# Attention step: mask and row extremum fused on VectorE, scores of the first four query blocks issued in pairs

## The chip, the cores and the metric

One core of a Trainium2 chip runs the whole layer. The metric is device time in microseconds, the median of the runs; the kernel before took 1771.34 us (three runs, 1770.96 to 1772.16).

## The reference

The reference computes one decoder layer in float32 for 1024 tokens and a model width of 1024. The part that matters here is differential causal attention with 8 heads. Each head has two maps (c = 0, 1) of 64 query and key channels and one value of 128 channels:

```python
sc = jnp.einsum('bhcqd,bhckd->bhcqk', q_blk, kt)       # q_blk: 128 queries, two maps
sc = jnp.where(k_pos[None, :] <= q_pos[:, None], sc, -jnp.inf)
p = jax.nn.softmax(sc, axis=-1)
p_diff = p[:, :, 0] - lam * p[:, :, 1]
o = jnp.einsum('bhqk,bhkv->bhqv', p_diff, vt)          # then RMSNorm per head
```

Before it come an RMSNorm and one wide projection, beside it a convolution, a pooling and three gates, and after it the output projection and a gated feed-forward block.

## The kernel before

Every float32 product is made of three fp32r products of high and low parts (the three PASSES: high by high, high by low, low by high). The program is written by hand for each engine: each engine has its own list of instructions in a fixed order, and semaphores tie the lists together. There is no planner; the order of the calls is the order on the engine.

Attention is a loop over heads, and within a head over eight steps, one for each query block i (a "row" of 128 queries that sees 128(i+1) keys). Head 0 and head 7 stand outside of the loop, heads 1 to 6 in it, two to a turn. Row i belongs to step i, but its stages are spread over several steps so that all engines work side by side.

- TensorE (`step_of`, and `scores` at L2440): the score products of row i; then the transposes of the difference of row i-1 (`diff_transposed`, L2348); then a quarter of a projection of the next head's keys or queries (`proj_part`, L2424, twelve products of 512 columns); then weights times values for row i-2 (L2462, L2464); then the transpose of the output y of row i-4 (L2348). A score product uses 64 rows of the array, rows 0 to 63 for map 0 and rows 64 to 127 for map 1; all the others use 128 rows.
- PSUM: map c has banks 2c and 2c+1. Rows 0 to 3 have at most 512 keys and use bank 2c alone; rows 4 to 7 use both, with three passes into the first and three into the second. `scores` waits for both exponentials of the row before (`exp_done`).
- VectorE (`step_of`): `masked` (L1669) waits for the scores and adds the triangular mask to the last 128 columns of both maps in one instruction, in place in PSUM, and waits for it; `maximum` (L1672) is called for each map and writes the negated row maximum over all 128(i+1) columns to `neg_max`. Then y of row i-3 (L1680), the low parts of the transposed row i-1 (L1559), and `difference` (L1657, L1658, L1662): reciprocals of the sums, a scale, and map 0 plus scale times map 1, into the tile `diff`. Splits of the next weights and low parts of projections (L1648) lie between the rows. The mask is a constant tile of 2 x 128 columns that GpSimd makes early in the kernel (L684, L685).
- ScalarE (`exps`, L1084): for each map the exponential of the scores plus `neg_max`, with the sum of the row from its accumulator, into `e_t`, which has two buffers (by i mod 2). Ahead of it in the same step ScalarE copies the high parts of the transposed row i-1.
- GpSimd computes the scale of the output norm from the sum of squares of u and moves values and outputs.

Of the kernel before, what the change touches and what calls it, by code (L numbers as in the profile page):

```python
# [12 lines left out]
P = 128  # L13
HALF = 512
EPS = 1e-6
MASKED = -1e30
WINDOWS = (2, 4, 8, 16)
# [55 lines left out]
def build(nc, x, g_pre_mix, w_in, b_gate, lambda_q1, lambda_k1, lambda_q2, lambda_k2, subln_g,  # L73
# [29 lines left out]
    with ctx:  # L103
# [72 lines left out]
        e_t = at("e_t", [P, 2, 2, S], F32, RF)  # L176
        diff = at("diff", [P, 2, S], F32, RF + 16384)
        gates_raw = at("gates_raw", [P, 2, S], F32, R2 + 16384)
# [35 lines left out]
        ident = const("ident", [P, P])  # L214
        mask = const("mask", [P, 2, P])
        bias_g = const("bias_g", [P, 3 * KT])
# [25 lines left out]
        def proj_weights(which, par, s):  # L242

            if which or not par:
                return ring[:, which, s, :]
            return k_other[s][:, :]

        def proj_bank(first, part):
# [33 lines left out]
        proj_done, proj_hi, proj_lo = sem("proj_done"), sem("proj_hi"), sem("proj_lo")  # L282
        scores_done, max_ready, exp_done = sem("scores_done"), sem("max_ready"), sem("exp_done")
        diff_ready = sem("diff_ready")
        u_lo_ready, u_ready = sem("u_lo_ready"), sem("u_ready")
# [344 lines left out]
        def _(pool):  # L630
# [16 lines left out]

            did(pool.memset(mask[0:1, 0, :], 1.0))
            did(pool.memset(ident[:, :], 0.0))
# [32 lines left out]

            for c in range(2):
                did(pool.memset(mask[:, c, :], 0.0))  # L684
                pool.affine_select(out=mask[:, c, :], in_=mask[:, c, :], compare_op=ALU.is_ge, fill=MASKED,  # L685
                                   base=0, pattern=[[-1, P]], channel_multiplier=1).then_inc(mask_ready, 1)
                pool.wait_ge(mask_ready, c + 1)
            store_v(TT - 2)
# [268 lines left out]
        def _(act):  # L957
# [120 lines left out]
            def exps(i, c):  # L1078

                w = P * (i + 1)  # L1080
                act.wait_ge(max_ready, t.at() * 2 + (c + 1))

                wait_for(act, diff_ready, t.at(-1))
                act.activation(e_t[:, i % 2, c, 0:w],  # L1084
                               ps[:, 2 * c:2 * c + 2, :].rearrange("p a b -> p (a b)")[:, 0:w], ACT.Exp,
                               bias=neg_max[:, i % 2, c:c + 1], accum_out=sums[:, i % 4, c:c + 1])\
                    .then_inc(exp_done, 1)
# [458 lines left out]
        def _(dve):  # L1546
# [106 lines left out]
            def difference(i, ahead=None):  # L1653
# [6 lines left out]
                if ahead:  # L1660
                    ahead()
                dve.scalar_tensor_tensor(diff[:, b, 0:w], e_t[:, b, 1, 0:w], d_scale[:, b:b + 1],  # L1662
                                         e_t[:, b, 0, 0:w], ALU.mult, ALU.add).then_inc(diff_ready, 1)

            def masked(i):

                dve.wait_ge(scores_done, t.at(1))
                block = ps[:, i // 4:i // 4 + 3:2, P * (i % 4):P * (i % 4 + 1)]
                did(dve.tensor_tensor(block, block, mask[:, :, :], ALU.add))  # L1669

            def maximum(i, c):
                dve.tensor_reduce(neg_max[:, i % 2, c:c + 1],  # L1672
                                  ps[:, 2 * c:2 * c + 2, :].rearrange("p a b -> p (a b)")[:, 0:P * (i + 1)],
                                  AX_X, ALU.max, negate=True).then_inc(max_ready, 1)

# [16 lines left out]
            def step_of(par, i, lag=0, first=False, last=False):  # L1692
                if not lag:
                    masked(i)
                    maximum(i, 0)
                    maximum(i, 1)
                if lag < 4 and not (first and i < 3):
# [36 lines left out]
            for half in range(2):  # L1734
                proj_lo_of(0, 1, half, first=True)
            dve.wait_ge(mask_ready, 2)
            for b in range(4):
                dve.wait_ge(v_stored[b], 16 * TT)
            for i in range(TT):
                step_of(0, i, first=True)  # L1740
            with turns(dve, (HEADS - 2) // 2, {n: 4, r: 4, p: 8, t: 16, trs: 40, step: 48}):
                for par in (1, 0):
                    for i in range(TT):
                        step_of(par, i)
# [574 lines left out]
        def _(pe):  # L2319
# [68 lines left out]
            for half in range(2):  # L2388
                pe.matmul(ps[:, 2 + half, :], mask[0:1, 0, :], g_pre_mix_b[0:1, HALF * half:HALF * (half + 1)],
                          start=True, stop=True).then_inc(g1_landed, 1)  # L2390
# [41 lines left out]
            def scores(par, i):  # L2432

                wait_for(pe, exp_done, t.at() * 2)
                for chunk in range(i // 4 + 1):
                    w = min(HALF, P * (i + 1) - HALF * chunk)
                    for n_pass, (a, b) in enumerate(PASSES):
                        for c in range(2):
                            rows = slice(HD * c, HD * (c + 1))
                            last = pe.matmul(ps[:, 2 * c + chunk, 0:w], qt[rows, par, a, P * i:P * (i + 1)],  # L2440
                                             kt[rows, par, b, HALF * chunk:HALF * chunk + w],
                                             start=n_pass == 0, stop=n_pass == 2)
                last.then_inc(scores_done, 1)

            def diff_transposed(i):
                pe.wait_ge(diff_ready, t.at())
                for b in range(i // 4 + 1):
                    blocks = min(4, i + 1 - 4 * b)
                    transpose_rows(b, diff[:, i % 2, HALF * b:HALF * b + P * blocks], blocks)

# [21 lines left out]
            def step_of(par, i, first=False):  # L2472
# [3 lines left out]
                if i == 4:  # L2476
                    pe.wait_ge(proj_lo, p.at(-2))
                scores(par, i)

# [305 lines left out]
```

## Time and profile before

| | |
|---|---|
| median of the runs | 1771.34 us |
| span of the profiled execution | 1769.8 us |
| TensorE busy | 1758.9 us (99%) |
| VectorE busy | 1151.7 us (65%) |
| ScalarE busy | 739.1 us (42%) |
| GpSimd busy | 250.7 us (14%) |

The page shows of the profiled execution its span, from the first to the last instruction; the runs are timed without a profile and from the outside, so that the two are not the same number. PE is TensorE, PEld its loading of weights, DVE is VectorE, ACT is ScalarE, POOL is GpSimd. L1672 is line 1672 of the kernel. A row of the timeline is a start in us from the beginning of the span, a duration, and what ran, where neighbours of one kind are put together (x6); a number in brackets is idle time before it and what ended it. A matmul's duration includes the way through the array, so that matmuls overlap and only the distance between starts tells how long a group takes.

### The profile page before, as it was taken

Reading aid. Unit: us, or ns where it says so; the run is one execution under the profiler, and the core shown is the slowest. Engines: PE = TensorE matmul, PEld = TensorE weight load, DVE = VectorE, ACT = ScalarE, POOL = GpSimd, SP = SyncE. Lnnn points to the kernel's source line nnn. Section 1 sums busy time; section 2 is a strip of 40 time slices with the busy share of each in tenths; the row PEclk is TensorE's granted clock in tenths of the full one; section 3 lists DMA queues with packets and bytes.
Section 4 is the critical chain, followed back from the end, with each engine's and each line's share of the span. In section 5 each row is a group of like instructions: output and inputs, shape, how many; then the busy total and the mean of one; then the engine's idle time right before and its main releaser. Section 6 shows DMA issues by size and latency. Waiting matters only on the chain.

```text
span 1769.8 us, 25045 instructions
## 1 busy us (share of the span) xinstructions
PE 1758.9 (99%) x8497; PEld 1455.0 (82%) x8497; DVE 1151.7 (65%) x1863; ACT 739.1 (42%) x1486; POOL 250.7 (14%) x557
## 2 busy tenths in 40 slices
PE   9999999999999999999999999999999999999998
PEld 7887888888888888888888888888888888888886
DVE  5328989999885774443465655776665655567676
ACT  5316666666743323443231123343333333344553
POOL 3221222222120001111100102101010000000011
PEclk9999999999999999999999999999999999999999
DMA  7421222222142222326735712223232322673443
GB/s 242 144 84 49 72 73 71 72 71 71 51 145 87 88 65 99 128 101 230 251 108 168 247 60 95 96 95 126 106 107 102 117 89 94 232 280 98 147 142 125
DMA packets 138041, 213.68 MB, mean 121 GB/s; under 512 B 7569, under 2 KB 94097, under 8 KB 136930
## 3 DMA queue, kind: packets, MB, share of 16 engines
q1 hardware_dynamic: 109200, 108.54, 19.4%
q0 software_dynamic: 28752, 104.04, 16.2%
q8 instruction: 46, 0.75, 0.2%
q14 instruction: 41, 0.34, 0.1%
q10 hardware_dynamic: 2, 0.00, 0.0%
HBM read 150.17 MB, written 62.39 MB: 120 GB/s over the span
## 4 chain that ended last, share of the span: by engine, by line
PE 98%; DVE 1%; issue 0%; ACT 0%; DMA 0%; POOL 0%; DVEq 0%; POOLq 0%; ACTq 0%
PE ps L2340 26%; PE ps L2672 22%; PE ps L2540 17%; PE ps L2728 12%; PE ps L2424 11%; PE ps L2440 4%; PE ps L2348 3%; PE ps L2462 2%; PE ps L2464 1%; DMA x_tile<-in_x_dram 0%; DVE pt L1559 0%; DVE ring L1559 0%; DVE neg_max L1672 0%; DVE ps L1669 0%; ACT e_t L1084 0%
## 5 line engine op out<-in xcount | busy, mean ns | idle before, releaser
L2728 PE MATMUL ps<-d_op 128*128 128x512 f32 x924 | 210.3, 389 | 0.1
L2728 PEld LDWEIGHTS ps<-d_op 128*128 128x128 f32 x924 | 173.3, 188 | 36.9 <-DVE d_op L1559 0.5
L2672 PE MATMUL ps<-s_op,t_op_T 128*128 128x512 f32 x720 | 169.9, 389 | 0.0
L2424 PE MATMUL ps<-xn,ring 128*128 128x512 f32 x672 | 167.1, 398 | 0.0
L2672 PEld LDWEIGHTS ps<-s_op,t_op_T 128*128 128x128 f32 x720 | 135.2, 188 | 28.0
L2424 PEld LDWEIGHTS ps<-xn,ring 128*128 128x128 f32 x672 | 122.5, 188 | 24.8 <-issue 0.2
L2540 PE MATMUL ps<-s_op,x_op_T 128*128 128x512 f32 x576 | 135.9, 389 | 0.0
L2540 PEld LDWEIGHTS ps<-s_op,x_op_T 128*128 128x128 f32 x576 | 108.1, 188 | 22.4
L2672 PE MATMUL ps<-hn,t_op_B 128*128 128x512 f32 x480 | 115.1, 389 | 0.0
L2672 PEld LDWEIGHTS ps<-hn,t_op_B 128*128 128x128 f32 x480 | 90.1, 188 | 18.7
L1084 ACT ACTIVATE e_t<-ps,neg_max 128x256 f32<-128x256 f32 (+7 forms) x128 | 94.1, 740 | 16.5 <-DVE neg_max L1672 15.1
L1559 DVE TENSOR_TENSOR t_op_B<-pair,t_op_B 128x512 fp32r<-128x512 f32 x60 | 41.4, 689 | 90.8 <-ACT t_op_B L963 90.8
L963 ACT ACTIVATE d_op<-rf_pieces 128x512 fp32r<-128x512 f32 x87 | 53.8, 629 | 106.6 <-PE ps L2728 101.1
L1559 DVE TENSOR_TENSOR d_op<-rf_pieces,d_op 128x512 fp32r<-128x512 f32 x87 | 59.3, 691 | 59.9 <-ACT d_op L963 59.9
L1672 DVE TENSOR_REDUCE neg_max<-ps 128x1 f32<-128x256 f32 (+7 forms) x128 | 91.0, 752 | 2.2
L2540 PE MATMUL ps<-xn,x_op_B 128*128 128x512 f32 x384 | 92.1, 389 | 0.0
L2340 PE MATMUL ps<-w_v,xn 128*128 128x512 f32 x384 | 90.5, 395 | 0.0
L2340 PE MATMUL ps<-w_o,ring 128*128 128x512 f32 x384 | 89.0, 391 | 0.0
L2340 PE MATMUL ps<-ya,ring 128*128 128x512 f32 x384 | 87.8, 389 | 0.0
L2340 PEld LDWEIGHTS ps<-w_v,xn 128*128 128x128 f32 x384 | 72.4, 190 | 15.1 <-DVE xn L1559 0.3
L2540 PEld LDWEIGHTS ps<-xn,x_op_B 128*128 128x128 f32 x384 | 72.1, 188 | 14.9
L2340 PEld LDWEIGHTS ps<-ya,ring 128*128 128x128 f32 x384 | 72.1, 188 | 14.9
(270 smaller groups left out, 3374.7 us busy)
## 6 DMA issues: line engine op xcount, KB each, us to landing
pair<-in_w_gate_up_dram SPq DMA_DIRECT2D x20, 1024.0 KB, 5.2
rf_pieces<-s_scratch SPq DMA_DIRECT2D x74, 256.0 KB, 2.7
x_pair<-in_w_in_dram SPq DMA_DIRECT2D x16, 1024.0 KB, 6.2
raw<-in_w_in_dram SPq DMA_DIRECT2D x26, 512.0 KB, 4.0
s_scratch<-gated_ff POOLq DMA_DIRECT2D x40, 256.0 KB, 2.5
gate_in<-gate_scratch POOLq DMA_DIRECT2D x18, 512.0 KB, 3.8
v_scratch<-v_out POOLq DMA_DIRECT2D x32, 256.0 KB, 2.6
vh<-v_scratch POOLq DMA_DIRECT2D x16, 512.0 KB, 5.3
```

The source lines that it names most:

```text
L963: return act.activation(dst, src, ACT.Copy, **kw)
L1084: act.activation(e_t[:, i % 2, c, 0:w], ps[:, 2 * c:2 * c + 2, :].rearrange("p a b -> p (a b)")[:, 0:w], ACT.Exp, bias=neg_max[:, i % 2, c ...
L1559: return dve.tensor_tensor(dst, src, hi.bitcast(F32), ALU.subtract)
L1672: dve.tensor_reduce(neg_max[:, i % 2, c:c + 1], ps[:, 2 * c:2 * c + 2, :].rearrange("p a b -> p (a b)")[:, 0:P * (i + 1)], AX_X, ALU.max, ...
L2340: last = pe.matmul(ps[:, bank, :], lhs, rhs, start=i == 0, stop=i == len(pairs) - 1)
L2348: last = pe.transpose(ps[:, TB[b], P * k:P * (k + 1)], src[:, P * k:P * (k + 1)], ident[:, :])
L2424: last = pe.matmul(ps[:, proj_bank(first, half), :], proj_weights(which, par, a)[:, P * k:P * (k + 1)], xn[:, b, k, HALF * half:HALF * (ha ...
L2440: last = pe.matmul(ps[:, 2 * c + chunk, 0:w], qt[rows, par, a, P * i:P * (i + 1)], kt[rows, par, b, HALF * chunk:HALF * chunk + w], start= ...
L2462: pe.matmul(ps[:, U_BANK, 0:2 * HV], pt[:, i % 2, HH, k, :], vh[:, par, :, k, :], start=k == 0, stop=k == i, skip_group_check=True)
L2540: last = pe.matmul(ps[:, bank, :], x_op[name][:, a, k, :], block(b, k), start=opens and (k, a, b) == (0, HH, HH), stop=(k, a, b) == (3, LL ...
L2672: last = pe.matmul(ps[:, bank, :], t_op[name][:, a, k, :], block(b, k), start=opens and (k, a, b) == (0, HH, HH), stop=(k, a, b) == (3, LL ...
L2728: last = pe.matmul(ps[:, DOWN_BANKS[product][i], :], d_op[:, g % 4, a, P * i:P * (i + 1)], d_op[:, g % 4, 2 + b, :], start=opens and (a, b ...
```

## The change

- Scores of rows 0 and 1 are issued at step 0, one behind the other, and those of rows 2 and 3 at step 2; steps 1 and 3 issue none. Rows 0 and 2 keep bank 2c, rows 1 and 3 now use bank 2c+1 (`score_row`). The wait for the exponentials of the row before stands ahead of each of the two, with the same value. `scores_done` is counted up after each row.
- `masked` and `maximum` become `minimum`, one VectorE instruction for each map: the scores plus a mask over the full width of the row, times -1, written back in place, and the minimum of the result as the negated maximum. ScalarE's exponential takes the negated scores with a scale of -1.
- The mask becomes one row of 1024 columns, zero but for the last 128; it takes the place in memory of the tile `diff`, and GpSimd makes it once the last normalised input rows have been read out of that place. The difference is written over the first map in `e_t`.
- A row of ones that TensorE reads in the first microseconds gets a tile of its own.

```diff
-        diff = at("diff", [P, 2, S], F32, RF + 16384)
+        mask = at("mask", [P, S], F32, RF + 16384)
...
+        def score_row(i, c):
+            first = 2 * c + (i % 2 if i < 4 else 0)
+            return ps[:, first:2 * c + 2, :].rearrange("p a b -> p (a b)")[:, 0:P * (i + 1)]
...
-            for c in range(2):
-                did(pool.memset(mask[:, c, :], 0.0))
-                pool.affine_select(out=mask[:, c, :], in_=mask[:, c, :], compare_op=ALU.is_ge, fill=MASKED,
-                                   base=0, pattern=[[-1, P]], channel_multiplier=1).then_inc(mask_ready, 1)
-                pool.wait_ge(mask_ready, c + 1)
+            pool.wait_ge(rows_ready, TT + 1)
+            did(pool.memset(mask[:, :], 0.0))
+            pool.affine_select(out=mask[:, S - P:S], in_=mask[:, S - P:S], compare_op=ALU.is_ge, fill=MASKED,
+                               base=0, pattern=[[-1, P]], channel_multiplier=1).then_inc(mask_ready, 1)
...
                 act.activation(e_t[:, i % 2, c, 0:w],
-                               ps[:, 2 * c:2 * c + 2, :].rearrange("p a b -> p (a b)")[:, 0:w], ACT.Exp,
-                               bias=neg_max[:, i % 2, c:c + 1], accum_out=sums[:, i % 4, c:c + 1])\
+                               score_row(i, c), ACT.Exp,
+                               bias=neg_max[:, i % 2, c:c + 1], scale=-1.0, accum_out=sums[:, i % 4, c:c + 1])\
...
-                dve.scalar_tensor_tensor(diff[:, b, 0:w], e_t[:, b, 1, 0:w], d_scale[:, b:b + 1],
+                dve.scalar_tensor_tensor(e_t[:, b, 0, 0:w], e_t[:, b, 1, 0:w], d_scale[:, b:b + 1],
                                          e_t[:, b, 0, 0:w], ALU.mult, ALU.add).then_inc(diff_ready, 1)
 
-            def masked(i):
-                dve.wait_ge(scores_done, t.at(1))
-                block = ps[:, i // 4:i // 4 + 3:2, P * (i % 4):P * (i % 4 + 1)]
-                did(dve.tensor_tensor(block, block, mask[:, :, :], ALU.add))
-
-            def maximum(i, c):
-                dve.tensor_reduce(neg_max[:, i % 2, c:c + 1],
-                                  ps[:, 2 * c:2 * c + 2, :].rearrange("p a b -> p (a b)")[:, 0:P * (i + 1)],
-                                  AX_X, ALU.max, negate=True).then_inc(max_ready, 1)
+            def minimum(i, c):
+                if c == 0:
+                    dve.wait_ge(scores_done, t.at(1))
+                    dve.sem_inc(scores_seen, 1)
+                w = P * (i + 1)
+                scores = score_row(i, c)
+                dve.tensor_tensor_reduce(out=scores, in0=scores, in1=mask[:, S - w:S], scale=-1.0, scalar=HIGHEST,
+                                         op0=ALU.add, op1=ALU.min, accum_out=neg_max[:, i % 2, c:c + 1])\
+                    .then_inc(max_ready, 1)
...
-                            last = pe.matmul(ps[:, 2 * c + chunk, 0:w], qt[rows, par, a, P * i:P * (i + 1)],
+                            last = pe.matmul(score_row(i, c)[:, HALF * chunk:HALF * chunk + w], qt[rows, par, a, P * i:P * (i + 1)],
...
-                scores(par, i)
+                if i >= 4 or i % 2 == 0:
+                    scores(par, i)
+                if i < 4 and i % 2 == 0:
+                    scores(par, i + 1)
```

## Rows read from the trace of the kernel before

**Rows 1.** The page: busy time of each engine; shares of the chain by engine.
```profile
PE 1758.9 (99%) x8497; PEld 1455.0 (82%) x8497; DVE 1151.7 (65%) x1863; ACT 739.1 (42%) x1486; POOL 250.7 (14%) x557
...
PE 98%; DVE 1%; issue 0%; ACT 0%; DMA 0%; POOL 0%; DVEq 0%; POOLq 0%; ACTq 0%
```

**Rows 2.** Busy time by stretch: head 0, and one head of the loop.
```profile
core 0: us, PE busy (x) PEld busy (x) DVE busy (x) ACT busy (x) POOL busy (x), PEclk, DMA share, GB/s
132.00:174.00 42.00, 41.04 (x257) 33.45 (x255) 37.30 (x80) 26.36 (x72) 7.40 (x20) 1.00 0.18 51
...
352.00:396.50 44.50, 44.39 (x286) 36.93 (x288) 40.36 (x91) 29.12 (x82) 9.96 (x27) 1.00 0.22 71
```

**Rows 3.** Waits of PE: us in total, times, longest.
```profile
PE ps L2440 <- ACT e_t L1084: 0.2, 1, 0.2
PE ps L2348 <- DVE diff L1662: 0.2, 1, 0.2
```

**Rows 4.** Timeline of PE, head 5 and start of 6: start us, duration us, what.
```profile
361.46 0.30 PE L2348 MATMUL ps<-ident,y_row 128*128 128x128 f32 x1
...
362.58 0.55 PE L2348 MATMUL ps<-ident,diff 128*128 128x128 f32 x3
...
367.52 0.66 PE L2348 MATMUL ps<-ident,diff 128*128 128x128 f32 x4
...
371.55 0.29 PE L2348 MATMUL ps<-ident,y_row 128*128 128x128 f32 x1
...
373.00 0.77 PE L2348 MATMUL ps<-ident,diff 128*128 128x128 f32 x5
...
383.44 0.29 PE L2348 MATMUL ps<-ident,y_row 128*128 128x128 f32 x1
...
385.25 0.98 PE L2348 MATMUL ps<-ident,diff 128*128 128x128 f32 x7
...
392.35 1.03 PE L2348 MATMUL ps<-ident,diff 128*128 128x128 f32 x8
393.13 0.71 PE L2424 MATMUL ps<-xn,k_other_hi 128*128 128x512 f32 x2
...
396.16 0.28 PE L2348 MATMUL ps<-ident,y_row 128*128 128x128 f32 x1
396.37 0.62 PE L2440 MATMUL ps<-kt,qt 64*128 64x256 f32 x6
396.93 0.33 PE L2348 MATMUL ps<-ident,diff 128*128 128x128 f32 x1
```

**Rows 5.** Timeline of DVE: row 3 of head 5, row 0 of head 6.
```profile
363.46 0.42 DVE L1669 TENSOR_TENSOR ps<-ps,mask 128x256 f32<-128x256 f32 x1
363.91 1.29 DVE L1672 TENSOR_REDUCE neg_max<-ps 128x1 f32<-128x512 f32 x2
...
366.63 0.75 DVE L1662 SCALAR_TENSOR_TENSOR diff<-e_t,d_scale 128x512 f32<-128x512 f32 x1
...
395.99 0.35 DVE L1662 SCALAR_TENSOR_TENSOR diff<-e_t,d_scale 128x128 f32<-128x128 f32 x1
```

**Rows 6.** Groups of instructions of DVE by line and shape: busy us, mean ns.
```profile
L1559 DVE TENSOR_TENSOR pt<-ps,pt 128x512 fp32r<-128x512 f32 x48 | 32.1, 683 | 0.0
L1669 DVE TENSOR_TENSOR ps<-ps,mask 128x256 f32<-128x256 f32 x64 | 27.3, 427 | 9.8 <-PE ps L2440 6.5 <-issue 3.1
...
L1672 DVE TENSOR_REDUCE neg_max<-ps 128x1 f32<-128x512 f32 x16 | 10.3, 685 | 0.3
...
L1662 DVE SCALAR_TENSOR_TENSOR diff<-e_t,d_scale 128x1024 f32<-128x1024 f32 x8 | 10.2, 1276 | 0.0
```

**Rows 7.** Groups of ACT by line and shape, attention alone.
```profile
L1084 ACT ACTIVATION_READ_ACCUMULATOR e_t<-ps,neg_max 128x1 f32 x126 | 24.7, 196 | 0.0
```

**Rows 8.** Timeline of POOL where the mask is made.
```profile
85.75 0.20 POOL L684 MEMSET mask<- 128x128 f32 x1
...
90.70 0.57 POOL L659 DMA_DIRECT2D v_scratch<-v_out  x1 [3.59 <-DVE v_out L1559]
```

More of the change, by code:

```diff
@@ L15 @@
 EPS = 1e-6
+HIGHEST = 3.0e38
 MASKED = -1e30
@@ L214, in build @@
         ident = const("ident", [P, P])
-        mask = const("mask", [P, 2, P])
+        ones = const("ones", [P, P])
         bias_g = const("bias_g", [P, 3 * KT])
@@ L283, in build @@
         scores_done, max_ready, exp_done = sem("scores_done"), sem("max_ready"), sem("exp_done")
+        scores_seen = sem("scores_seen")
         diff_ready = sem("diff_ready")
@@ L646, in rstd_of @@
                                    ALU.pow).then_inc(rstd_ready, 1)
-            did(pool.memset(mask[0:1, 0, :], 1.0))
+            did(pool.memset(ones[0:1, :], 1.0))
             did(pool.memset(ident[:, :], 0.0))
@@ L1693, in step_of @@
                 if not lag:
-                    masked(i)
-                    maximum(i, 0)
-                    maximum(i, 1)
+                    minimum(i, 0)
+                    minimum(i, 1)
                 if lag < 4 and not (first and i < 3):
@@ L1735, in _ @@
                 proj_lo_of(0, 1, half, first=True)
-            dve.wait_ge(mask_ready, 2)
+            dve.wait_ge(mask_ready, 1)
             for b in range(4):
@@ L1740, in _ @@
                 step_of(0, i, first=True)
-            with turns(dve, (HEADS - 2) // 2, {n: 4, r: 4, p: 8, t: 16, trs: 40, step: 48}):
+            with turns(dve, (HEADS - 2) // 2, {n: 4, r: 4, p: 8, t: 16, trs: 40, step: 32}):
                 for par in (1, 0):
@@ L2388, in _ @@
             for half in range(2):
-                pe.matmul(ps[:, 2 + half, :], mask[0:1, 0, :], g_pre_mix_b[0:1, HALF * half:HALF * (half + 1)],
+                pe.matmul(ps[:, 2 + half, :], ones[0:1, :], g_pre_mix_b[0:1, HALF * half:HALF * (half + 1)],
                           start=True, stop=True).then_inc(g1_landed, 1)
@@ L2448, in diff_transposed @@
                     blocks = min(4, i + 1 - 4 * b)
-                    transpose_rows(b, diff[:, i % 2, HALF * b:HALF * b + P * blocks], blocks)
+                    transpose_rows(b, e_t[:, i % 2, 0, HALF * b:HALF * b + P * blocks], blocks)
             def weighted_values(par, i, newer):
```

## The prediction

> **What bounds the kernel now.** I read the page first. TensorE is busy 99% of the span and is 98% of the chain that ended last [rows 1]; every other engine is covered, so a change pays only if it takes time out of TensorE's own stream or out of one of its few waits. Then the busy times by stretch: in one head of the attention loop (44.5 us) TensorE is busy 44.39, VectorE 40.36, and the granted clock is 1.00 throughout [rows 2]. VectorE is therefore second by only four microseconds and lies in a loop with TensorE: scores, mask, maximum, exponential, difference, transposes. The table of waits shows that TensorE waits for this loop almost nowhere; two waits of 0.2 us, for the exponentials and for the difference, are all that is booked on it [rows 3]. They belong to head 0: the first 42 us of attention hold 0.96 us of idle TensorE [rows 2].
>
> "Busy" hides something, which the timeline of TensorE shows. Score products use 64 rows of the array, everything around them 128. In step 1 the transpose of y starts at 396.16, the six products of 256 columns at 396.37, the next transpose at 396.93 [rows 4]: 0.77 us, though one transpose is 0.10 (eight of them fill 392.35 to 393.13) and three passes of 256 columns are 0.36 (below). So some 0.31 us is entering and leaving. Steps 5 and 7 show that this is paid once per group and not per bank: there twelve products in two banks follow each other, 371.55 to 373.00 = 1.45 us with a second half of 256 columns and 383.44 to 385.25 = 1.81 us with one of 512, against 1.12 us for the first half alone (361.46 to 362.58) [rows 4]. A second group thus costs 0.33 us at 256 columns and 0.69 us at 512, so 0.36 us for three passes of 256 columns.
>
> **The change, part by part.**
> *Scores in pairs.* Step 1 loses 0.77 - 0.10 = 0.67 us and step 0 gains 0.33: net 0.34. Step 3 loses 1.12 - 0.10 = 1.02 and step 2 gains 0.69: net 0.33. Per head 0.67 us, over eight heads 5.4 us, all on the path. The wait ahead of the pair is the old one of its first row (exponentials of the row before), so nothing is queued behind a new wait; the odd row has its own banks, so the products of row 1 don't touch what VectorE is reducing.
>
> *One VectorE instruction per row and map.* Before, a row costs the mask addition, 0.45 us from its start to the start of the first reduction (363.46 to 363.91), and two reductions [rows 5]. After, it is two fused instructions, each reading scores from PSUM and the mask from SBUF and writing back. An addition of that kind is in the trace: 427 ns for 256 columns in place, 683 ns for 512, a plain reduction 685 ns for 512 [rows 6]. So I price the pass itself as the reduction. Bringing the minimum out is not shown on VectorE. Bounds: from below nothing beyond the pass; from above 0.20 us each, the mean of ScalarE's accumulator read [rows 7]; far above, a second cycle per column (the second rival). I take 0.09 us, nearer to the lower end, as a read can overlap the next instruction's start. A row then saves 0.45 - 0.18 = 0.27 us, a head 2.2 us of 40.4. This is not on the path by itself; it pays for what follows.
>
> The Trainium skill ("VectorE: DVE Perf Modes", section on two Vector instructions with no wait between them) says that an operation with an accumulator output is two instructions, the main one and a read. No VectorE row here shows one; by it a row would hold four instructions in place of three, and at ScalarE's 0.20 us the saving would be 0.05 us a row, in place of 0.27.
>
> *What is late next.* Without the scores of row 1 ahead of them, the transposes of row 0 are wanted 0.67 us sooner: 4.58 - 0.67 = 3.91 us behind those of row 7 (392.35 to 396.93 before), while the difference of row 0 ended 395.99 + 0.35 = 396.34, 3.99 behind [rows 4, 5]. With some 0.1 us for the semaphore it is 0.2 late, unless the 0.27 us of row 0 and row 7 reach it. The second place is row 3: its difference ended 366.63 + 0.75 = 367.38, its transposes began at 367.52, 0.14 us spare [rows 4, 5]. TensorE comes there 0.67 us sooner; rows 0 to 3 give 4 x 0.27 = 1.1 us, but part of their chain is ScalarE and GpSimd, which don't get faster. I book 0.1 us of new waiting per head, from 0 to 0.35.
>
> *Head 0* is bound by VectorE's chain in its first steps, so there 0.27 us a row for four rows counts, 1.1 us; bounds 0.5 (mask saving of two rows) and 1.7 (0.96 us of idle time gone and 0.67 of TensorE's own).
>
> *At nothing:* the wide zero mask on GpSimd. A memset of 128 columns took 0.20 us; eight times that is 1.6 us at most, and GpSimd then idled 3.59 us before its next store [rows 8]; without that cover up to 1.6 us of a store would slip, still long before head 0. The difference in place writes as many columns as before; its buffer is overwritten by exponentials that ScalarE issues behind the copies of a later transpose, so no wait is added. The sign in the exponential is a constant of the instruction.
>
> **Sum.** 7 x (0.67 - 0.10) + 1.1 = 5.1 us. The profiled execution shows a span of 1769.8 us; it becomes 1764.7. The median of the runs, 1771.34, lies 1.5 us above that span, and I keep this: 1766.2 us.
>
> **Rivals.**
> 1. *TensorE's saving turns into waits.* If reading the minimum costs 0.2 us or more, VectorE gains nothing, and the two late places eat 0.2 to 0.5 of the 0.67 us per head; the same result would come if the second row of a pair paid the entry again. For: 0.14 us spare at row 3. Against: 0.45 us is surely gone from each row, and the two-bank groups of steps 5 and 7. Time: 8 x 0.17 to 8 x 0.4 saved at the far end, 1768.1 to 1771; around 1770.
> 2. *The fused instruction is slow, and VectorE becomes the bound.* An addition, a scaling and a running minimum per column could take two cycles. Additions cost (683 - 427)/256 = 1.0 ns a column [rows 6]; a head has 2 x 4608 columns, 9.2 us more, less the 2.2 us of above: VectorE at 47.4 us a head, with one to four microseconds of its present idle time left 48.4 to 51, against 44.4 now. Over eight heads 32 to 53 us: about 1805. It decides from the price at which VectorE's head passes TensorE's: 40.4 - 3.6 (the masks) + 16x = 43.7, x = 0.43 us above a reduction. The Trainium skill ("Vector Engine (DVE) Microarchitecture Reference", points that are easy to get wrong) says that the scalar-tensor-tensor shape with two non-bf16 SBUF sources runs at half throughput, with no port left for the accumulator. The difference is of this shape with two such sources, without an accumulator, and took 1276 ns for 1024 columns [rows 6]: not halved; and the scores are in PSUM.
> 3. *More than I book:* no waits at all and head 0 freed wholly: 7 x 0.67 + 1.7 = 6.4, with 0.3 for the roughness of the readings 6.7: 1764.6. This is the end of the gain, since TensorE can't give more than its entries.
>
> **Numbers.** Forecast, with rival 3: 0.66. Rival 1: 0.21. Rival 2, in all sizes: 0.13. A measurement here can tell 0.2% (3.5 us) from no change: faster beyond 1767.8, slower beyond 1774.9. Faster 0.67 (all but a little of the first case and some of rival 1), same 0.21, slower 0.12. The range goes from 1764.0, just below the end of the gain, to 1772.5, which takes in rival 1 and the start of rival 2.
>
> **What would show it.** Six score products followed by six more without a gap at steps 0 and 2, and the transposes of rows 0 and 2 directly behind that of y. Head period 43.8 us in place of 44.4. The fused instruction about 0.7 us at 512 columns and VectorE near 38 us a head. Wrong if: TensorE shows waits on the difference above 0.2 us a head (rival 1), or the fused instruction takes about 2 ns a column (rival 2), or the time outside attention moves by more than 0.5 us.

## The result and the profile after

The changed kernel is slower. Its median is 1775.76 us (10 runs, 1774.82 to 1776.78) against 1771.52 for the kernel before on the same chip: ratio 1.0023, 95% interval 1.0015 to 1.0031. The forecast was 1766.2 and the range 1764.0 to 1772.5: the measured time lies above its upper end. The profiled execution has a span of 1774.8 us, 5.0 more than before.

The page's busy row and the shares of the chain come first; they answer to [rows 1].

```profile
PE 1758.3 (99%) x8497; PEld 1456.9 (82%) x8497; DVE 1131.0 (64%) x1927; ACT 735.0 (41%) x1486; POOL 250.2 (14%) x555
...
PE 93%; DVE 3%; issue 2%; POOL 1%; ACT 1%; DMA 0%; POOLq 0%; DVEq 0%; ACTq 0%
```

VectorE is 20.7 us less busy, as wanted. But TensorE's share of the chain fell from 98% to 93%, and "issue", time in which an engine waited for nothing that the profile shows, rose from 0 to 2%. Where that lies is seen from the time between the starts of the transposes of row 7 of one head and the next (timeline of TensorE; heads 1 to 6 are in the loop, two to a turn, and heads 3 and 5 begin a new turn):

| head | 1 | 2 | 3 | 4 | 5 | 6 | 7 |
|---|---|---|---|---|---|---|---|
| before, us | 44.35 | 44.26 | 44.81 | 44.26 | 44.74 | 44.27 | 43.81 |
| after, us | 44.33 | 44.11 | 48.37 | 44.06 | 48.39 | 44.09 | 42.57 |

Heads 3 and 5 lose 3.56 and 3.65 us; head 7 gains 1.24, the rest of the loop 0.55 together, head 0 0.43 (to its row 7). The sum is 5.0 lost, the whole difference of the spans. From row 7 of head 7 to the end it is 1289.4 us in both kernels, so nothing moved outside of attention.

Busy times by stretch (columns as in [rows 2]), for head 4 and head 5:

```profile
306.30:350.40 44.10, 43.88 (x286) 36.96 (x285) 37.01 (x94) 28.70 (x82) 10.02 (x28) 1.00 0.23 72
350.40:398.80 48.40, 45.89 (x286) 38.15 (x285) 37.97 (x102) 28.81 (x82) 10.00 (x28) 0.96 0.21 66
```

VectorE needs 37 to 38 us a head, not 40.4. In head 5 TensorE has 2.5 us of idle time and the granted clock falls to 0.96. Waits of TensorE in heads 1 to 7, where the kernel before shows none:

```profile
PE ps L2353 <- DVE pt L1565: 3.6, 2, 1.8
PE ps L2353 <- DVE e_t L1668: 2.3, 8, 0.5
```

Timeline of VectorE where head 5 begins, and the chain of waits of the same stretch (start, duration, what):

```profile
349.48 0.28 DVE L1565 TENSOR_TENSOR y_out<-ps,y_out 128x128 fp32r<-128x128 f32 x1
354.11 0.30 DVE L1678 CUSTOM_DVE_ANT_0 ps<-ps,mask 128x128 f32<-128x128 f32 x1 [4.34 <-issue]
354.32 0.14 DVE L1678 DVE_READ_ACCUMULATOR2_ANT neg_max<- 128x1 f32 x1
354.32 0.33 DVE L1678 CUSTOM_DVE_ANT_0 ps<-ps,mask 128x128 f32<-128x128 f32 x1
```

```profile
349.76 1.84 issue
351.60 0.06 DVEq L51
351.66 2.29 issue
353.95 0.02 DVEq L1675
353.97 0.14 issue
354.11 0.25 DVE ps L1678
```

VectorE stands for 4.34 us at the loop's turn: 1.84 us to the loop's first instruction (L51), 2.29 more to its second (L1675). The kernel before stands 1.59 and 1.53 us there. The transfers in 256 to 264 us, around the other turn, are nothing but code:

```profile
q14 instruction: 3, 0.02, 1.1%
```

TensorE behind the turn of head 5:

```profile
354.13 0.23 PE L2469 MATMUL ps<-vh,pt 128*128 128x128 f32 x1
356.17 0.33 PE L2353 MATMUL ps<-ident,y_row 128*128 128x128 f32 x1 [1.81 <-DVE pt L1565]
357.01 0.32 PE L2353 MATMUL ps<-ident,e_t 128*128 128x128 f32 x1 [0.51 <-DVE e_t L1668]
357.09 4.58 PE L2429 MATMUL ps<-xn,ring 128*128 128x512 f32 x12
```

It idles 1.81 and 0.51 us, and then twelve products take 4.58 us that take 3.00 at a granted clock of 1.00 (experiment 1). Busy times by stretch for these products (the granted clock is the third number from the end):

```profile
357.09:361.50 4.41, 4.41 (x13) 3.47 (x14) 2.36 (x10) 2.51 (x8) 0.93 (x3) 0.61 0.00 0
```

A mean of 0.61 says that for most of this stretch TensorE had the lower of its two clocks (1.2 GHz, 0.50); ahead of it (from 353.90) and from 361.50 on it is 1.00. Waits and slower products are 2.32 + 1.58 = 3.90 us of the 4.12 that head 5 is longer than in the same kernel without the gap.

The fused instruction itself, by shape (busy us, mean ns), answers to [rows 6]:

```profile
L1678 DVE CUSTOM_DVE_ANT_0 ps<-ps,mask 128x1024 f32<-128x1024 f32 x16 | 19.3, 1248 | 6.5 <-PE ps L2445 6.5
L1678 DVE DVE_READ_ACCUMULATOR2_ANT neg_max<- 128x1 f32 x128 | 18.2, 142 | 0.0
...
L1678 DVE CUSTOM_DVE_ANT_0 ps<-ps,mask 128x512 f32<-128x512 f32 x16 | 10.7, 711 | 0.0
```

(1248 - 711)/512 = 1.05 ns a column, and the read of the accumulator is an instruction of its own, but the next operation starts with it (354.32 twice above).

### The profile page after: what moved, and what is told of

Read it like the earlier page. It is cut to its first block, busy times and chain, and to the rows that moved or that the text cites. A ratio compares the mean times of both kernels' runs of the same rounds, so it can differ in the third digit from the quotient of the medians.

```text
span 1774.8 us, 25115 instructions
## 1 busy us (share of the span) xinstructions
PE 1758.3 (99%) x8497; PEld 1456.9 (82%) x8497; DVE 1131.0 (64%) x1927; ACT 735.0 (41%) x1486; POOL 250.2 (14%) x555
## 4 chain that ended last, share of the span: by engine, by line
PE 93%; DVE 3%; issue 2%; POOL 1%; ACT 1%; DMA 0%; POOLq 0%; DVEq 0%; ACTq 0%
PE ps L2345 26%; PE ps L2680 21%; PE ps L2548 17%; PE ps L2736 11%; PE ps L2429 8%; PE ps L2353 3%; PE ps L2445 3%; PE ps L2467 2%; PE ps L2469 1%; DVE pt L1565 1%; POOL o_scale L727 0%; DVE e_t L1668 0%; DVE d_scale L1664 0%; DVE ring L1565 0%; DVE u_row L1693 0%
## 5 line engine op out<-in xcount | busy, mean ns | idle before, releaser
L1678 DVE CUSTOM_DVE_ANT_0 ps<-ps,mask 128x256 f32<-128x256 f32 (+7 forms) x128 | 94.5, 780 | 22.5 <-PE ps L2445 13.8
```

What stands on the lines that cost most here:

```text
L1678: dve.tensor_tensor_reduce(out=scores, in0=scores, in1=mask[:, S - w:S], scale=-1.0, scalar=HIGHEST, op0=ALU.add, op1=ALU.min, accum_out=n ...
```

## The experiments

The theory that the traces gave: the turn of VectorE's loop waits for code. In the compiled programs an instruction has 64 bytes, and the instruction queue moves 8 KB at a time, 128 instructions. The loop's body has 318 instructions before and 334 after, and the change puts 15 more ahead of it. A place is an instruction's number within its 8 KB, from 0 to 127. Where the 8 KB boundaries lie isn't in the profile; I assumed that the changed loop's first instruction is the last of its 8 KB (place 127), since its second came 2.29 us after it. The kernel before then starts at place 112, and all other places follow by counting. Experiments 1 to 4 bear the assumption out: with the two kernels they leave only 126 and 127 for it, if a loop is fetched anew where it touches four pieces and stays where it touches three. The rival: the fused instruction or the pairs make the gap themselves.

### 1. The changed kernel, loop shifted by two instructions

```diff
             dve.wait_ge(mask_ready, 1)
+            for _ in range(4):
+                dve.wait_ge(mask_ready, 1)
```

> The changed kernel with four more waits on VectorE ahead of the first head, on a semaphore value that is long there; they put two more instructions ahead of the loop over the heads and change nothing in it. Theory (placement of the code): in the changed kernel VectorE stands 4.33 and 4.34 us at the two loop turns (the kernel before: 1.59 and 1.53), because the loop body's first instruction is the last of one 8192-byte fetch and its second stands in the next. With the body moved to the head of a fetch, the gaps fall to 1.0 to 1.7 us, the transposes of row 7 of heads 3 and 5 come about 44.1 to 44.9 us after those of the head before (48.37 and 48.39 in the changed kernel), TensorE's granted clock is 0.99 or more in these heads, and the time is 1766.5 to 1769. Rival (the fused instruction or the pairs make these gaps, whatever the placement): gaps above 4 us and 1775 to 1776.5.

In the compiled program four such waits make two instructions. Measured: 1768.18 us (ratio to before 0.9980, 0.9971 to 0.9989). Heads 3 and 5 took 44.29 and 44.27 us. Timeline of VectorE at both turns, and the twelve products of TensorE behind the second:

```profile
257.25 0.28 DVE L1565 TENSOR_TENSOR y_out<-ps,y_out 128x128 fp32r<-128x128 f32 x1
257.45 0.29 DVE L1678 CUSTOM_DVE_ANT_0 ps<-ps,mask 128x128 f32<-128x128 f32 x1
...
345.60 0.28 DVE L1565 TENSOR_TENSOR y_out<-ps,y_out 128x128 fp32r<-128x128 f32 x1
345.79 0.29 DVE L1678 CUSTOM_DVE_ANT_0 ps<-ps,mask 128x128 f32<-128x128 f32 x1
```

```profile
356.95 3.00 PE L2431 MATMUL ps<-xn,ring 128*128 128x512 f32 x12
```

No gap is left, not even the 1.5 us of before: the theory was right on the time and too careful on the gap. Two instructions that do nothing are worth 7.6 us.

### 2. The kernel before, loop shifted to place 127

```diff
             dve.wait_ge(mask_ready, 2)
+            for _ in range(31):
+                dve.wait_ge(mask_ready, 2)
```

> The kernel before with 31 more waits on VectorE ahead of the first head, on a semaphore value that is long there: 15 more instructions in the queue, so that the loop's body begins at the place in VectorE's code that it has in the changed kernel. Theory (placement of the code): the two gaps at the loop turns go from 1.59 and 1.53 us to above 4, the two heads to about 48.5 us, and the time is 1777 to 1780. Rival (the changed instructions make the gaps): 1771 to 1772, as the kernel before.

Measured: 1779.78 us (ratio 1.0044, 1.0031 to 1.0057); heads 3 and 5 48.39 and 49.71. The added waits also delay head 0 by 1.6 us (its first transpose starts at 132.34 in place of 130.77), since VectorE is not idle there. First turn on VectorE:

```profile
259.78 0.28 DVE L1559 TENSOR_TENSOR y_out<-ps,y_out 128x128 fp32r<-128x128 f32 x1
263.99 0.43 DVE L1669 TENSOR_TENSOR ps<-ps,mask 128x256 f32<-128x256 f32 x1 [3.93 <-issue]
```

The old instructions make the long gap as well once their loop begins there, so the rival is ruled out. (The profiled execution was the longest of the five, 1782.19 us. Its second turn costs more than its first because TensorE had the lower clock for longer behind it: the granted clock is 0.66 in 356.5 to 366.5 us and 0.83 in 264 to 274 us.)

### 3. The kernel before, loop shifted to lie in three fetches

```diff
+            for _ in range(34):
+                dve.wait_ge(lam_landed, 16 * 5)
             for half in range(2):
                 proj_lo_of(0, 0, half, first=True)
```

> The kernel before with 17 more instructions on VectorE where it stands idle (ahead of the first projection), so that its loop begins one instruction behind the start of an 8192-byte fetch and lies in three of them instead of four. Nothing else is changed. Theory (the loop's code is fetched again at every turn only where it does not lie in three fetches): no fetch on the instruction queue between about 240 and 440 us, the gaps of 1.59 and 1.53 us at the two turns go, heads 3 and 5 take 44.3 us (44.81 and 44.74 before), and the time is 1770.3 to 1771. Rival (a turn costs 1.5 us in this kernel wherever its code lies): 1771.3 to 1772.

Measured: 1770.31 us; heads 3 and 5 44.32 and 44.33. The ratio, 0.9994 (0.9985 to 1.0003), does not tell the two kernels apart, but the heads do. VectorE at the second turn:

```profile
346.36 0.28 DVE L1559 TENSOR_TENSOR y_out<-ps,y_out 128x128 fp32r<-128x128 f32 x1
346.56 0.42 DVE L1669 TENSOR_TENSOR ps<-ps,mask 128x256 f32<-128x256 f32 x1
```

Between 256 and 440 us the instruction queue moved nothing, whereas in the kernel before, in the same stretch, it moved

```profile
q14 instruction: 10, 0.08, 0.1%
```

which is also where the 8 KB come from (0.08 MB in 10 packets).

### 4. The changed kernel, loop at place 53

Edit as in 3, with 108 waits (54 instructions) on the changed kernel.

> The changed kernel with 54 more instructions on VectorE ahead of the first projection (most of them where VectorE stands idle): the loop begins at place 53 of an 8192-byte fetch and reaches into a fourth. Theory: the code is fetched again at each turn, but the first fetch holds 75 instructions of the loop, so that only the first fetch is waited for and not two: gaps of 1.3 to 2.0 us as in the kernel before, heads 3 and 5 at 44.4 to 45.0 us, and 1768.5 to 1770 (up to 1 us more if the waits themselves delay the first head). Rival A (every fetch anew costs over 4 us in the changed kernel): 1775. Rival B (no fetch anew, gaps of 0.9): 1768.2 as the shifted changed kernel.

Measured: 1770.53 us; heads 3 and 5 45.29 and 45.21. VectorE at the first turn (from 256 to 440 us the instruction queue moved 11 packets):

```profile
260.01 0.30 DVE L1678 CUSTOM_DVE_ANT_0 ps<-ps,mask 128x128 f32<-128x128 f32 x1 [2.82 <-issue]
```

The code was fetched anew, as expected of a loop in four fetches, and VectorE waited for code once and not twice: the chain of waits has 2.56 us to the first instruction and 0.05 to the second. But the gap is 2.82 us where I expected 1.3 to 2.0, and the time is 0.5 us above my upper end. The chains of waits show most of the reason; here the kernel before and then this run (the first line is the branch back, the last the loop's first instruction):

```profile
257.16 0.06 DVEq L50
...
258.54 1.48 issue
260.02 0.06 DVEq L50
```

```profile
256.27 0.07 DVEq L51
...
257.19 2.56 issue
259.75 0.06 DVEq L51
```

From branch to first instruction it is 2.86 us before and 3.48 here, and in between one packet of code starts before and two here. Also VectorE, which still works off what it was given ahead of the branch, covers 1.38 us of it before (until 258.54) and only 0.92 here (until 257.19). Why two packets go out at this place is not shown. TensorE idled 0.29 and 0.51 us behind the turn, and its granted clock stayed at 1.00.

Places and gaps together:

| | place | 8 KB pieces touched | q14 packets, 256 to 440 us | gaps at the turns, us |
|---|---|---|---|---|
| before | 112 | 4 | 10 | 1.59, 1.53 |
| after | 127 | 4 | 10 | 4.33, 4.34 |
| 2, before | 127 | 4 | 10 | 3.93, 3.86 |
| 4, after | 53 | 4 | 11 | 2.82, 2.78 |
| 1, after | 1 | 3 | 0 | none |
| 3, before | 1 | 3 | 0 | none |

### 5. The pairs alone, and the fused instruction alone

The pairs on the kernel before; the odd row has banks of its own, chosen so that the mask's two blocks lie side by side:

```diff
-                scores(par, i)
+                if i >= 4 or i % 2 == 0:
+                    scores(par, i)
+                if i < 4 and i % 2 == 0:
+                    scores(par, i + 1)
...
+        def score_row(i, c):
+            if i < 4:
+                return ps[:, 2 * (i % 2) + c, 0:P * (i + 1)]
+            return ps[:, 2 * c:2 * c + 2, :].rearrange("p a b -> p (a b)")[:, 0:P * (i + 1)]
```

> The kernel before with the paired score products alone (the two products of a row pair lie in banks of their own as in the change; the mask addition and the two row maxima are as before). VectorE's code has the length of the kernel before, so its loop is placed as there. As the prediction booked the pairs: 0.67 us a head less on TensorE, 1771.5 less 5, 1766 to 1767. Theory now (the pairs shorten TensorE's steps 1 to 3, but these steps end on the VectorE chain that runs over the scaled row, the difference and the sum of the row): most of it comes back as waiting at the transposes, 1769.5 to 1771.5. Rival (pairs make the loop turns long): above 1775.

The kernel of experiment 1 with `scores(par, i)` at every step again:

> The changed kernel with the score products in the order of before (each row's pair of products at its own step), so the fused mask and minimum alone, with the four added waits, so that VectorE's loop is placed as in the shifted changed kernel. As the prediction booked it: VectorE is 0.27 us a row shorter, which lies beside TensorE's work except in the first head and the head outside the loop: 1769.5 to 1771.5. Rival (the fused instruction holds the rows up): slower than the kernel before, above 1772. Second rival (the shorter VectorE row alone carries the gain of the heads): 1767 to 1769.

Measured: the pairs alone 1772.07 us (ratio 1.0003, 0.9994 to 1.0011), no gain, 0.6 us above what I expected; the fused instruction alone 1768.76 (0.9984, 0.9975 to 0.9993), the second rival's range. With the pairs on top it is 1768.18 (experiment 1). So at equal placement the fused instruction gives 1.6 us (from the 1770.31 of experiment 3; the kernel before stood at 1771.66 and 1771.52 beside the two; by the spans of the profiled executions it is 1.2) and the pairs 0.6. Differences of this size lie within the intervals of the ratios; the heads carry the argument. Heads, in us:

| head | 1 | 2 | 3 | 4 | 5 | 6 | 7 |
|---|---|---|---|---|---|---|---|
| before, three fetches | 44.33 | 44.25 | 44.32 | 44.27 | 44.33 | 44.29 | 43.81 |
| pairs alone | 44.56 | 44.53 | 45.03 | 44.56 | 45.05 | 44.53 | 42.75 |
| fused alone | 44.19 | 44.19 | 44.19 | 44.19 | 44.19 | 44.19 | 43.60 |
| both (1) | 44.29 | 44.07 | 44.29 | 44.06 | 44.27 | 44.09 | 42.55 |

The pairs take 1.05 us out of head 7 and nothing worth naming out of a head in the loop. (Some 0.4 of the 1.05 is a shift: row 7 of a head now waits for one more row of the next head's scores, 7.51 us behind row 6 in place of 7.10, and behind head 7 there is no next head. The rest, 0.65, is the booked saving.) TensorE's waits in the pairs alone, heads 1 to 7:

```profile
PE ps L2354 <- DVE diff L1668: 1.6, 5, 0.6
PE ps L2446 <- ACT e_t L1090: 1.2, 6, 0.2
```

### 6. What eats the pairs in the loop

Steps 2 and 3 of head 4 on VectorE in experiment 1:

```profile
312.04 0.28 DVE L1693 TENSOR_TENSOR u_row<-ps,u_lo 128x128 f32<-128x128 f32 x1
...
314.20 0.35 DVE L1686 SCALAR_TENSOR_TENSOR y_row<-u_row,o_scale,g_sub 128x128 f32<-128x128 f32 x1 [0.63 <-POOL o_scale L728]
...
315.31 0.62 DVE L1668 SCALAR_TENSOR_TENSOR e_t<-e_t,d_scale 128x384 f32<-128x384 f32 x1
315.84 1.22 DVE L1565 TENSOR_TENSOR ring<-raw,ring 128x1024 fp32r<-128x1024 f32 x1
316.98 0.28 DVE L1693 TENSOR_TENSOR u_row<-ps,u_lo 128x128 f32<-128x128 f32 x1
...
319.14 0.35 DVE L1686 SCALAR_TENSOR_TENSOR y_row<-u_row,o_scale,g_sub 128x128 f32<-128x128 f32 x1 [0.36 <-POOL o_scale L728]
...
320.37 0.75 DVE L1668 SCALAR_TENSOR_TENSOR e_t<-e_t,d_scale 128x512 f32<-128x512 f32 x1
```

and the transposes that follow on TensorE:

```profile
321.26 0.65 PE L2355 MATMUL ps<-ident,e_t 128*128 128x128 f32 x4 [0.23 <-DVE e_t L1668]
```

From one u_row to the next it is 4.94 us: a square on ScalarE and three operations on GpSimd (o_scale) to y_row, then the difference, then the weight split `ring` of 1.22 us. The difference ends 0.13 to 0.14 us ahead of its transposes in rows 2 and 3, that is, they wait for it. Row 3's transposes come 5.20 us behind row 2's; in the kernel before and in the fused instruction alone it is 4.93. Two edits try the two suspects: y_row's wait, and the split.

```diff
-                if lag < 4 and not (first and i < 3):
-                    y_of((i - 3) % TT)
...
+                if lag < 4 and not (first and i < 3):
+                    y_of((i - 3) % TT)
                 if lag < 3 and not (first and i < 2):
                     sum_u((i - 2) % TT)
```

> The shifted changed kernel (the same two instructions more ahead of VectorE's loop, put where VectorE stands idle anyway) with one more edit: in every step the scaling that makes y_row stands behind the difference and the weight splits, just ahead of the sum for u_row, and no longer ahead of the difference. Theory (the pairs' saving turned into waiting at the transposes of rows 2 and 3, because y_row's wait on GpSimd's o_scale, 0.63 and 0.36 us there, stands ahead of the difference): the slack of 0.13 us at rows 2 and 3 grows, the transposes of rows 1 to 2 and 2 to 3 are 0.23 us (odd heads) and 0.2 to 0.3 us closer, a head takes 43.6 to 43.9 us instead of 44.06 and 44.29, and the time is 1765.5 to 1767. Rival (the exponentials, not y_row, end last at these rows): heads at 44.0 to 44.3 and 1768 to 1768.5. Other rival (y_row itself comes late for its transposes): above 1768.5.

> The paired score products alone on the kernel before, with the scaling that makes y_row moved behind the difference and the splits as in the run above; VectorE's code is placed as in the kernel before. Theory: the old mask addition and maximum leave VectorE 40 us busy of 44.5 in a head, so rows 2 and 3 still wait, but less: heads at 44.1 to 44.4 us instead of 44.53 and 44.56, 1769.5 to 1771. Rival (without the fused instruction the pairs cannot gain at all): 1771.8 to 1772.3, as the pairs alone.

Measured: 1767.60 us for the changed kernel with y_row moved (0.9977, 0.9968 to 0.9986), 1777.76 for the pairs alone with y_row moved (1.0035, 1.0021 to 1.0049). The first misses its range by 0.6, with heads at 44.09 to 44.15: the odd ones gained 0.15 to 0.2, the even ones nothing, and head 7 lost 0.3. Heads 1 to 7 together take 307.57 us, against 307.62 in experiment 1, so a gain from this edit is not shown. The second is wrong in sign: 5.7 us slower than without the edit, heads at 45.44 to 45.61. The reason stands in VectorE's row 3, here in the first of them,

```profile
318.29 0.55 DVE L1565 TENSOR_TENSOR pt<-ps,pt 128x384 fp32r<-128x384 f32 x1
319.29 0.17 DVE L1663 RECIPROCAL rsums<-sums 128x2 f32<-128x2 f32 x1 [0.46 <-ACT e_t L1090]
```

and here in the second:

```profile
321.44 0.35 DVE L1686 SCALAR_TENSOR_TENSOR y_row<-u_row,o_scale,g_sub 128x128 f32<-128x128 f32 x1
...
324.77 0.17 DVE L1663 RECIPROCAL rsums<-sums 128x2 f32<-128x2 f32 x1 [0.45 <-ACT e_t L1090]
```

y_row used to stand in time that VectorE had to wait anyway, for the exponentials. Moved out of it, its 0.27 us come on top (in the second kernel rows 2 and 3 come 0.22 and 0.26 us later behind the row before, rows 4 to 6 some 0.1 to 0.2), and the wait only changes its name from GpSimd to ScalarE. My single limit was two chains of nearly equal length, 4.94 us through o_scale, 5.11 through the exponentials (difference 314.70 to 319.81 in the first of the two). Both hold the split.

```diff
-                    if i == 2 and not last:
+                    if i == 6 and not last:
                         split_weights(0, par)
```

on ScalarE and VectorE alike.

> The shifted changed kernel with one more edit: the weight split that stands in step 2 behind the difference (1.22 us on VectorE, 1.06 on ScalarE) stands in step 6 instead, on both engines; y_row stands where the change has it. Theory (two chains end nearly together at row 3, one through GpSimd's o_scale and y_row, 4.93 us a row, and one through minimum, exponentials, difference, split and the next minimum, 5.11 us when y_row is moved; both hold the split of step 2): without the split in it the transposes of rows 2 to 3 are 4.9 us apart (5.20 in the shifted changed kernel, 4.88 in head 7, which has no split), the slack of row 3 grows from 0.13 to 0.4 or more, a head takes 43.5 to 43.9 us, and the time is 1765.3 to 1766.8. In step 6 the split falls into gaps of 0.93 us on VectorE and 1.11 on ScalarE. Rival (TensorE itself cannot run the paired order faster): tr rows 2 to 3 stays at 5.2 us and 1768. Other rival (the split in step 6 delays row 7): above 1768.5.

> The run above with y_row moved behind the difference too. Theory: row 2 of the odd heads gains the 0.23 us that it gained in the kernel with y_row alone moved, three heads; row 3 has its slack already: 0.3 to 0.8 us below the run above, 1764.8 to 1766.2. Rival (y_row in its new place adds 0.27 us to the rows that the exponentials end): as the run above or up to 0.5 us slower.

> The paired score products alone on the kernel before (old mask addition and maximum, VectorE's code placed as there), with the split of step 2 moved to step 6 on both engines. Theory: the pairs did nothing alone (1772.07) because rows 2 and 3 wait for VectorE; with 1.1 us less there they gain: heads at 43.9 to 44.3 us instead of 44.53 and 44.56, 1768.5 to 1770.5. Rival (the pairs need the fused instruction: VectorE's rows 4 to 7, now with the split among them, end last): 1771.5 or more.

> The fused mask and minimum alone (score products in the order of before, VectorE's loop placed to lie in three fetches), with the split of step 2 moved to step 6 on both engines. It is the control of the run with the pairs and the moved split. Theory (the moved split gives back the pairs' saving and has none of its own: without the pairs TensorE is busy 44.19 of 44.19 us in a head): heads stay at 44.1 to 44.3 us and the time is 1768.2 to 1769.3, as the fused instruction alone (1768.76). Rival (the moved split shortens the heads by itself): 1766 to 1767.5.

Measured: the changed kernel with the split in step 6: 1765.71 us (0.9966, 0.9954 to 0.9979), the fastest here and ahead of both kernels. With y_row moved as well 1767.15 (0.9977, 0.9967 to 0.9987), against my expectation: rows 6 and 7 of a head are 7.8 to 7.9 us apart in place of 7.6 (the rival's mechanism, at three times its price). The pairs alone with the split in step 6: 1769.68 (0.9990, 0.9981 to 0.9999). The control, without the pairs: 1769.43 (0.9986, 0.9977 to 0.9995), 0.7 above the fused instruction alone and 0.1 above my range: with the split in step 6 row 7 comes 0.1 us later in each head. The fastest kernel shows row 3 freed on VectorE (u_row now waits for ScalarE's copy of TensorE's product) and on TensorE (the difference ends 0.42 us ahead of its transposes), and a head filled by TensorE:

```profile
314.64 0.29 DVE L1693 TENSOR_TENSOR u_row<-ps,u_lo 128x128 f32<-128x128 f32 x1 [0.47 <-ACT u_lo L969]
...
318.05 0.75 DVE L1668 SCALAR_TENSOR_TENSOR e_t<-e_t,d_scale 128x512 f32<-128x512 f32 x1
```

```profile
319.22 0.65 PE L2355 MATMUL ps<-ident,e_t 128*128 128x128 f32 x4
```

```profile
304.60:348.30 43.70, 43.70 (x286) 36.84 (x285) 37.47 (x98) 28.90 (x82) 9.99 (x27) 1.00 0.22 72
```

Rows 2 to 3 are 4.92 us apart (314.30 to 319.22; 5.20 in experiment 1), and heads take 43.71 (even) and 43.95 to 44.00 (odd). The difference to the control, 3.7 us, is what the pairs give where VectorE lets them; against the fused instruction alone, which doesn't pay for the moved split, it is 3.1.

## Why the prediction was wrong

*The step that failed is the list of what the change costs.* "The change part by part" counts the instructions that VectorE executes and prices "at nothing" a memset, a buffer and a sign. It does not count the code: 15 instructions more ahead of the loop, 16 more in it. They moved the loop's first instruction from place 112 to 127, and at each of the two turns the time until VectorE goes on grew by 2.8 us; TensorE lost 8.2 us by it in heads 3 and 5 (48.37 and 48.39 against 44.29 and 44.27), 1.6 us of each head by the lower clock behind its idle time. Experiments 1 to 3 show it with the instructions changed and unchanged. The sign was in the rows: 3.1 us of "issue" ahead of the mask addition [rows 6], in two waits at the turns, were idle time of VectorE that no work explained, and I passed over them.

The Trainium skill ("Runtime: NRT & Kernel Launch", section "Instruction fetch mechanics") says that a taken branch to code outside the present window of two blocks waits for a fetch. The runs agree on the mechanism: 3 packets of code at a turn, and none where there is no gap. The Trainium skill gives a block 16 KiB, 256 instructions. The runs don't agree with that size: no alignment of blocks of 256 instructions puts the loops that were fetched anew (before, after, 2 and 4) into three blocks and the others (1 and 3) into two. Here the packets have 8 KB, and a loop in three of them stayed.

*The pairs: right in size, wrong in "what is late next".* The entries saved are there: the even heads of the fastest kernel take 43.71 us against 44.29 and 44.30 in its control, 0.6 where 0.67 was forecast, and head 7 shows 0.65. But "I book 0.1 us of new waiting per head" should have been about 0.6: at equal placement heads 1 to 6 take 44.18 us on average with the pairs and 44.19 without, and the pairs gave 0.6 us in all and not 4. Of the two late places named, row 0 cost nothing (3.95 us behind row 7, where 3.91 was reckoned), and row 3 (0.14 us spare) cost 0.3 in every head of the loop; row 4 cost 0.1 and row 2 of the odd heads 0.25. The price was wrong because I took VectorE's saving of 0.27 us a row to shorten the chain there in full. It does so in part: row 3 comes 5.20 us behind row 2 with the fused instruction and 5.38 without it, but from one u_row to the next it is 4.94 in both. One chain goes through GpSimd and the other through the exponentials, and the difference comes when the later of the two allows. This is rival 1's outcome by another mechanism; its condition, a read that costs 0.2 us, is not met.

*The fused row: right.* VectorE needs 37.5 us a head where "near 38" was forecast; the read of the accumulator is 142 ns long and lies beside the next operation. Rival 2 is out: 1.05 ns a column. The fused instruction gave 1.6 us, 0.5 in head 0 (38.64 us from its first transposes to those of row 7, 39.12 in experiment 3), where 1.1 was booked together with the pairs, and some 0.1 in each head of the loop, where nothing was.

*Of the signs named:* waits on the difference are 2.3 us in seven heads, above 0.2 a head, but two of 0.5 us stand behind the turns; at equal placement it is 1.3, just under 0.2. The head period is 44.1 (even) and 44.3 (odd), not 43.8. The time outside attention did not move. Without the placement the change would have stood at 1768.18, inside the range and 2 us above the forecast, but that would have been partly luck: 1.2 us of it are the turns of the kernel before (1771.52 to 1770.31), which the forecast did not count. At equal placement the change gives 2.1 us (1770.31 to 1768.18) where 5.1 were booked.

*What stays open:* why a turn at place 53 sends for two packets of code ahead of the loop's first instruction and one at place 112 for a single one; and why the odd heads of the fastest kernel take 0.25 us more than the even ones; it lies in row 2, and is gone where y_row is moved.

## What to carry to other kernels

A loop on an engine's queue has a place in its code, and any edit ahead of it or in it moves that place: look for idle time marked "issue" at the loop's turns and for packets on the instruction queue before comparing two versions, and place the loop alike in both. A saving on the engine that bounds the kernel counts only up to the next chain that ends at the same wait, and two chains of nearly equal length have to be shortened in what they share (here the split, 2.5 us) and not in the one that the profile happens to name (y_row: no gain that is shown, and 5.7 us lost on the pairs alone). An operation that stands in a wait that is there anyway costs nothing; moved out of it, it does.

## What the runs showed of the hardware beyond that

- Two instructions without effect made 7.6 us (1775.76 to 1768.18), because the loop of 334 instructions then touches three 8 KB pieces of code and not four, by the places counted above.
- Idle time of TensorE was paid twice: behind waits of 1.81 and 0.51 us the granted clock was 0.61 over twelve products, which took 4.58 us in place of 3.00. Behind waits of 0.29 and 0.51 us (experiment 4) it stayed at 1.00.
- A fused addition, scaling and running minimum over scores in PSUM took 1.05 ns a column, as an addition alone does [rows 6].
